# Loading the sample's rows between two layers in two halves of columns

## What is computed

```
for l in range(2):
    h = rmsnorm(x, mix_norm[l])
    parts = split(h @ w_in[l])                 # attention, SSD, mLSTM inputs
    x = x + concat([attention, ssd, mlstm]) @ w_out[l]
    h = rmsnorm(x, ffn_norm[l])
    aff = softmax(h @ router[l])               # 16 experts
    gate, idx = top_k(aff.T, rows // 8)        # each expert chooses its rows
    ye = (silu(h[idx] @ w_gate) * (h[idx] @ w_up)) @ w_down * gate
    x = x + scatter_add(ye, idx)               # per sequence
```

## Time and profile before

| | us |
|---|---|
| median of 3 runs | 2253.24 |
| lowest and highest run | 2251.92 and 2255.58 |
| the profiled execution | 2253.64 |
| its span, first to last instruction | 2252.2 |
| layer 1's first transposes begin | 1127.94 |

### The profile page before, as it was taken

The page is one execution under the profiler, slowest core; times in us unless marked ns, Lnnn a source line. Parts: engine busy times, 40 slices in busy tenths (PEclk is TensorE's granted clock), DMA queues, the critical chain, the costliest instruction groups (busy, mean ns, idle before and its releaser), DMA issues.

```text
span 2252.2 us, 32436 instructions
## 1 busy us (share of the span) xinstructions
PE 2211.3 (98%) x12450; PEld 1575.5 (70%) x12450; DVE 1250.6 (56%) x2415; ACT 611.3 (27%) x1409; POOL 565.2 (25%) x660
## 2 busy tenths in 40 slices
PE   8999999999999999999999999999999999999998
PEld 6557578874446888887775575888744468887786
DVE  3555466587766345555236544666876654555442
ACT  3221233484332111111142212335733311111111
POOL 1103454154311211111111044541443111111111
PEclk9999999999999999999999999999999999999999
DMA  4002122633658988878540111335346589878883
GB/s 159 21 20 75 57 94 94 155 122 107 207 158 296 340 300 287 289 268 286 144 138 22 32 63 56 112 111 118 110 135 208 179 287 345 288 268 297 292 290 76
DMA packets 179540, 388.84 MB, mean 173 GB/s; under 512 B 12181, under 2 KB 63897, under 8 KB 179386
## 3 DMA queue, kind: packets, MB, share of 16 engines
q1 hardware_dynamic: 162042, 344.68, 44.5%
q0 software_dynamic: 15264, 41.95, 7.5%
q10 hardware_dynamic: 2080, 0.13, 0.1%
HBM read 329.77 MB, written 56.96 MB: 172 GB/s over the span
## 4 chain that ended last, share of the span: by engine, by line
PE 84%; DVE 8%; ACT 3%; DMA 2%; issue 1%; POOL 1%; SPq 0%; DVEq 0%; ACTq 0%; POOLq 0%
PE ps L1976 82%; DVE TMP L1347 2%; DVE TMP L1788 1%; DVE SCR L1347 1%; DMA MID<-w_up 1%; PE ps L1995 1%; POOL SCR L764 1%; ACT SCR L1133 1%; DVE HT L1347 1%; DVE SCR L1793 1%; ACT SCR L1092 1%; DMA HT<-h_sample,idxs 1%; DVE TMP L1793 0%; PE ps L2028 0%; ACT SCR L1153 0%
## 5 line engine op out<-in xcount | busy, mean ns | idle before, releaser
L1976 PE MATMUL ps<-MID,HT 128*128 128x512 f32 (+3 forms) x2560 | 679.4, 490 | 4.7 <-DVE HT L1347 3.0
L1976 PEld LDWEIGHTS ps<-HT,MID 128*128 128x128 f32 x4096 | 553.9, 190 | 17.1 <-issue 15.2
L1976 PE MATMUL ps<-HT,MID 128*128 128x160 f32 (+1 forms) x4096 | 557.4, 298 | 1.6 <-DVE HT L1347 1.4
L1976 PEld LDWEIGHTS ps<-MID,HT 128*128 128x128 f32 (+1 forms) x2560 | 298.7, 156 | 287.5 <-issue 247.5
L1976 PE MATMUL ps<-RING,HT 128*128 128x256 f32 (+2 forms) x1760 | 387.3, 389 | 4.8 <-DVE SCR L1347 3.0
L1976 PEld LDWEIGHTS ps<-RING,HT 128*128 128x128 f32 (+1 forms) x1760 | 313.1, 190 | 62.8 <-issue 16.1
L1976 PE MATMUL ps<-HT,RING 128*128 128x512 f32 (+1 forms) x960 | 349.7, 522 | 0.0
L1976 PEld LDWEIGHTS ps<-HT,RING 128*128 128x128 f32 x960 | 180.2, 190 | 153.3 <-issue 145.2
L1918 DVE STREAM_TRANSPOSE HT<-HT 32x256 f32<-32x256 f32 x576 | 251.0, 436 | 18.4
L1356 DVE SCALAR_TENSOR_TENSOR HT<-HT,ps 128x160 f32<-128x160 f32 (+1 forms) x128 | 40.9, 319 | 396.8 <-ACT HT L1309 377.3
L927 POOL DMA_INDIRECT y_prompt<-SCR,idxp x32 | 50.4, 1574 | 583.3 <-ACT SCR L1319 542.8
(11 more groups left out here) (284 smaller groups left out, 2109.5 us busy)
## 6 DMA issues: line engine op xcount, KB each, us to landing
MID<-w_gate SPq DMA_DIRECT2D x32, 2048.0 KB
MID<-w_up SPq DMA_DIRECT2D x32, 2048.0 KB
MID<-w_down SPq DMA_DIRECT2D x32, 2048.0 KB
RING<-w_in SPq DMA_DIRECT2D x20, 1024.0 KB, 5.3
SCR<-cs_rows SPq DMA_DIRECT2D x20, 1024.0 KB, 5.2
p_rows<-SCR SPq DMA_DIRECT2D x12, 768.0 KB
HT<-p_rows SPq DMA_DIRECT2D x48, 192.0 KB, 3.6
y_sample<-RING SPq DMA_DIRECT2D x16, 512.0 KB, 4.4
```

Source lines behind the costliest of these rows:

```text
L1976: return pe.matmul(out, a, b, start=start, stop=stop)
```

## The change

The sample's loads into layer 1 are cut into halves of columns, 256 KB each (`x_half_load`). The first half-scatter of the last expert now counts on `gathered[2]`, a semaphore that till then counted gathers, and the second on `scattered_s` as before. SyncE waits for the first half-scatter, issues the first halves of chunks 2 to 6, waits for the second half-scatter, and then issues the rest: the second halves of chunks 2 to 6, and both halves of chunks 7 to 9, chunk by chunk. ScalarE's square waits for both halves (32 counts for a chunk instead of 16), GpSimd gets a wait for `gathered[2]` at the two places where it waited for `scattered_s`, and `counts` follows. In layer 0 the chunks are loaded whole, as before.

```diff
             return {"x": 16 * layer, "scatter": ..., 
-                    "halves": 16 * (E + 1) * layer,
-                    "gather": [16 * layer * len(range(j, E, 3)) for j in range(3)],
+                    "x_halves": max(0, 32 * layer - 16), "halves": 16 * E * layer,
+                    "gather": [16 * layer * (len(range(j, E, 3)) + (j == 2)) for j in range(3)],
...
+                    def x_half_load(c, hf):
+                        cols = slice(hf * 512, (hf + 1) * 512)
+                        sp.dma_start(XN[c][:, cols], layer_x(c)[:, cols]).then_inc(x_loaded[c if c < 4 else 2 + c // 2], 16)
...
                         for c in range(1, NP):
                             x_load(c)
+                        for c in range(NP, NC):
+                            x_load(c)
                     else:
+                        sp.wait_ge(gathered[2], seen["gather"][2])
+                        for c in range(NP, NP + 5):
+                            x_half_load(c, 0)
                         sp.wait_ge(scattered_s, seen["halves"])
-                    for c in range(NP, NC):
-                        x_load(c)
+                        for c in range(NP, NC):
+                            if c >= NP + 5:
+                                x_half_load(c, 0)
+                            x_half_load(c, 1)
                     ring_load(1)
                     ring_load(2)
...
                         pool.wait_ge(scattered_s, seen["halves"])
+                        pool.wait_ge(gathered[2], seen["gather"][2])
...
-                                                        compute_op=ALU.add, bounds_check=2 * SEQS[1] - 1).then_inc(scattered_s, 16)
+                                                        compute_op=ALU.add, bounds_check=2 * SEQS[1] - 1
+                                                        ).then_inc(scattered_s if hf else gathered[2], 16)
...
-                        pool.wait_ge(scattered_s, seen["halves"] + 16 * (E + 1))
+                        pool.wait_ge(scattered_s, seen["halves"] + 16 * E)
+                        pool.wait_ge(gathered[2], seen["gather"][2] + 16 * (len(range(2, E, 3)) + 1))
...
                     def square(c):
-                        act.wait_ge(x_loaded[c if c < 4 else 2 + c // 2], (seen["x"] + 16) * (1 if c < 4 else 2))
+                        own = seen["x"] + 16 if c < NP else seen["x_halves"] + (32 if layer else 16)
+                        act.wait_ge(x_loaded[c if c < 4 else 2 + c // 2], own * (1 if c < 4 else 2))
```

More of the change, by code:

```diff
@@ L510, in counts @@
         def counts(layer):
-            return {"x": 16 * layer, "scatter": 16 * E * layer, "halves": 16 * (E + 1) * layer,
-                    "gather": [16 * layer * len(range(j, E, 3)) for j in range(3)],
+            return {"x": 16 * layer, "x_halves": max(0, 32 * layer - 16), "scatter": 16 * E * layer, "halves": 16 * E * layer,
+                    "gather": [16 * layer * (len(range(j, E, 3)) + (j == 2)) for j in range(3)],
                     "quad": [16 * layer * len(range(j, NQ, 2)) for j in range(2)]}
```

## The result

The changed kernel takes 2258.37 us (median of 17 runs, 2256.45 to 2261.11), the kernel before 2254.23 in the runs beside it (17 runs, 2251.01 to 2257.59). The ratio is 1.0019, with a 95% interval of [1.0013, 1.0026]: **4.1 us slower**, above the range that was predicted. The profiled execution took 2257.74 us around a span of 2256.3 (before: 2253.64 and 2252.2). The page's engine table of the kernel after (busy time, share of the span, instructions) answers the earlier trace rows: TensorE is busy 1.5 us longer with the same instructions.

What follows compares the result with a forecast made beforehand. TensorE was taken as the bound. Chunk 2's later landing adds 0.5 us to the profiled 2253.64, giving 2254.1, or 2253.7 us on the median's scale (step's bounds 2253.1 to 2254.7); the range was 2251.3 to 2257.1.

Steps and rivals of the forecast that it cites:

- What bounds the kernel: Seam between the layers: TensorE, busy 98%, is the bound; no sample load in the chain; earlier landing saves at most 0.09 us.
- Later costs TensorE microsecond for microsecond: Chunk 2's load at the seam: almost no slack, so each microsecond of later landing costs TensorE one microsecond.
- When SyncE may start: SyncE's split scatter wait: first half-scatter lands 6.3 us after issue, at 1130.5; five loads issue by 1132.9, 0.47 us each.
- When chunk 2 is whole: Chunk 2's landing behind five first halves: 1131.5 + 0.43 + 6 x 0.67 + 1.2 = 1137.15, 0.65 us later than before.
- the price of a half: Flow of each 256 KB half ahead of chunk 2's landing: 0.67 us, from expert weights' 392 GB/s.
- the scatter's rest: Second half-scatter's remaining hold on the DMA engines after the halves' flow starts at 1131.5: 0.43 us.
- the upper end: Slow bound for chunk 2's landing: halves at 325 GB/s, 0.81 us each, landing at 1138.0, 1.5 us later.
- The third term: Chunk 2's load, from its last packet to its landing: 1.2 us.
- The rejected rival: Each half at the seam takes as long as a whole, 1.29 us: chunk 2 at 1140.9, +4.3, 2257.6; chance 0.03 including non-overlapping halves.
- Chunks 3 to 9 needed nothing: Layer 1's later chunks: chunk 3 squared long after landing, later ones come sooner; no gain, as TensorE doesn't pause after 1143.03.
- The scatter was not held up: Rival at the second half-scatter: early halves delay its last packets, up to +2.5 us, 2255.7; chance 0.08.
- The weight loads moved back: Two input-weight loads behind SyncE's sample loads: issued 1.4 us later, covered by 28 us before first use at 1180.0.

Runs made afterwards that it cites:

- e5: Changed kernel with only chunk 2's first half sent ahead, then its second half and chunks 3 to 9 whole; 0.0 us against the kernel before, ratio 0.9996.
- e10: Changed kernel with the five first halves sent ahead as one transfer of 1.25 MB; +4.6 us against the kernel before, ratio 1.0018.
- e1: Changed kernel with five unread products on the identity put into TensorE's pause ahead of chunk 2's transposes; +2.7 us against the kernel before, ratio 1.0008.
- e2: Changed kernel with only the first halves of chunks 2 and 3 sent ahead, not of five chunks; +0.9 us against the kernel before, ratio 1.0002.
- e12: Changed kernel with the same order of sixteen halves, but all issued only after the second half-scatter; +6.1 us against the kernel before, ratio 1.0027.
- e4: Changed kernel with layer 1's halves read as gapless 256 KB blocks of the sample's input; +3.3 us against the kernel before, ratio 1.0013.
- e7: Kernel before, whole loads, with chunks 4 and 5 loaded ahead of chunks 2 and 3; +4.4 us against the kernel before, ratio 1.0018.
- e14: Changed kernel with all halves after the second half-scatter, each 64 whole rows instead of 128 half rows; +7.7 us against the kernel before, ratio 1.0036.
- e3: Changed kernel with nothing sent ahead: all sixteen halves go after the second half-scatter, chunk by chunk; +0.1 us against the kernel before, ratio 0.9994.
- e11: Chunk 2's first half alone sent ahead, plus chunk 3 squared before chunk 2's scaling and scaled before its copies; -1.7 us against the kernel before, ratio 0.9991.

## Why the prediction was wrong

**What bounds the kernel: right.** No load stood in the chain, and an earlier landing is worth nothing: e5 brought chunk 2 0.42 us earlier and ran in the time of before. "Later costs TensorE microsecond for microsecond" was too cheap (below).

**When SyncE may start: nearly right.** The half-scatter landed 6.66 us after its issue, not 6.3, and the flow began 1.1 behind that: + 0.5 on the predicted start. The issues came slower, 9.48 us for 16, or 0.59 each, against 0.47; one took 1.31. There is no sign that they decided: five halves' bytes were not through until about T + 13.0, and the sixth had been issued at T + 9.86.

**When chunk 2 is whole: this step failed.** "+ 0.65" was + 3.09 for the square, and the excess of 2.4 lies in two terms of the sum:
- start + 0.5, as above;
- **the price of a half, + 1.9**: the sum had the scatter's rest of 0.43 and six halves at 0.67, 4.45 together; they took about 6.3. Even the upper end, six at 0.81, gave only 5.3.

The third term, 1.2 from the last packet to the landing, came out at 1.3.

The price of a half was that of a steady flow, the 392 GB/s of a weight transfer. The halves did reach such a flow, 408 GB/s from 1139 on, but only behind the six that chunk 2 waits for; those flowed at 232 to 299. Signs of a slow start were there: the 2 us ahead of the weight transfer's row, 205 GB/s at a DMA share of 0.71; and, in a row that the prediction used for the start of the flow alone, 123 GB/s with the engines full from 1134.0. By that row and the three shown behind it, before's first 512 KB had moved by about 1136.0 and landed 0.5 later. So the 1.2 of the sum was 0.5 of landing and 0.7 of slow start; that it fits after's 1.3, where the parts of the last half end 2.4 us apart, is luck.

**The rejected rival was nearest.** "If only a half took as long as a whole, 1.29", with chunk 2 at 1140.9 and + 4.3, had a share of 0.03. The first six halves cost 1.05 of flow each. Its landing was too late by 1.3 us (T + 15.38 measured, 16.7 by the rival), and it had no clock in it, which added 2.67 at the seam; that its total, 2257.6, came closest to the measurement is in part luck, as the two errors pull against each other.

The Trainium skill, "DMA: Bandwidth & Descriptors", section "Rules for kernel authors", advises coalescing many small transfers into one large one. The runs agree in part: a half ahead of chunk 2 cost 0.86 to 1.17 us, more than half of a whole's 1.30, but one transfer of 1.25 MB in place of five was no better (e10, 16.15 against 15.46). Its section "Anatomy of one DMA" has a fit for transfers issued by GpSimd; by it six halves paid in turn would take 15.6 us, an estimate. Here, issued by SyncE, the six took 8.7, from the first issue at 1129.50 to the landing at 1138.20.

**The pause was costed one to one, with no term for the clock.** Where TensorE pauses for 2.59 us and then for 1.93, the clock's halving adds 2.67 at the seam; e1 takes 2.65 of it away by filling the pause. Nothing in before shows a half clock at the seam, and from before's mean clock of 0.999 it was taken that the clock plays no part. It played none in before; the prediction didn't ask what a longer pause would do to it.

**The other steps held.** Chunks 3 to 9 needed nothing. The scatter was not held up: SyncE's second wait ended at T + 8.5 to 8.8 in e2 and e5, 8.81 before; in after the scatter's last count comes at 8.79, as in before. The weight loads moved back by 3.6 us, not 1.4, as SyncE's issues came slower (T + 16.20; before 12.62 by the earlier trace rows), and nobody waited for them: their first use is at about 1184. The early start was worth something, 1.6 us (e12 against after), but of a loss that the order had made.

**What stays open.** Why a flow of halves is slow for its first six or so, and whole rows only for their first: not the gaps or the source (e4), not the 2 KB piece by itself (408 GB/s later), and not simply the number of transfers (e10). Whether SyncE's one long issue, during which the share of the DMA engines fell to 0.65, has a part in it was not tested; e12 is slow without one. And the seam's own sum, 5.75 us, is above the 4.1 measured [2.9 to 5.9 by the interval], as e7's (2.62 + 2.7) is above 4.4. In the two profiled executions layer 0 was 1.4 us shorter in after, which makes up most of the distance to the spans' 4.1; the traces are of one execution each, and the seam's clock differs between executions.

## What to carry to other kernels

Starting a load earlier is worth nothing if it also puts others' data ahead of the bytes that are wanted next: count what stands in the queue ahead of the last byte of the first consumer, and price it by rows from the start of such a queue, not by a steady flow. Where TensorE would pause for more than it does now, ask for the price of the clock as well, and look for useless work to fill the pause. And where the chain shows two engines' order between a landing and TensorE, change the order first: that gave 1.7 us here, and the load nothing.

## What was not expected of the hardware

- The first six loads of 256 KB in 2 KB pieces took about 1.05 us of flow each, those behind them 0.64 (408 GB/s, after); whole rows of 4 KB pieces reached 401 GB/s within 2 us (before). The 16 parts of such a half end up to 2.5 us apart; those of a whole chunk 2 in before 0.4.
- A transfer into 64 partitions ran at 218 GB/s with the DMA engines full, one into 128 at 404 (e14, before).
- A pause of 2.3 to 2.6 us of TensorE, a short piece of work and another pause of 1.93 went with a granted clock of 0.50 from about the second pause on, worth 2.7 us (after, e7). The pause of 1.93 alone did so in one profiled execution (e3) and not in two others (before, e5).
- In after, e1, e2, e5 and e10 one of SyncE's early issues, and in e4 two, took 1.03 to 1.31 us instead of 0.43, beside an instruction transfer of 16 KB; in e11, with one early half, none took over 0.64 among the first. That the one causes the other was not tested.
